# Attention loop: the last three query units' projections in one or two chunks a step, and their later stages moved

## The chip, the cores and the metric

The kernel runs on one core of a Trainium2 chip. Its time is the device time of one execution in microseconds (us); the figure quoted is the median of the runs. The core has a matmul engine (TensorE, PE in the profile), a vector engine (VectorE, DVE), an activation engine (ScalarE, ACT), a general engine (GpSimd, POOL) and a queue engine that issues the transfers (SyncE, SP). Each runs its own instructions strictly in the order written, and they meet at semaphores.

## What is computed

Two layers on a sequence of 512 tokens with 1024 features. The first has a gated short convolution, the second differential attention on a shared key and value set; each ends with a squared-ReLU MLP. The change lies in the attention of the second layer:

```python
q = rms_norm((h @ w_q).reshape(b, s, 8, 2, 64), q_norm)          # 8 heads, two components of 64
for i in range(s // 128):                                        # 4 blocks of 128 queries
    sc = einsum('bqhcd,bkhcd->bhcqk', qb, kb) * scale            # both components
    p = softmax(where(causal, sc, NEG_INF))
    a = p[:, :, 0] - lam * p[:, :, 1]
    out = einsum('bhqk,bkhe->bqhe', a, vb)
o = rms_norm(o, sub_norm) * (1 - lam_init)
return o.reshape(b, s, 1024) @ w_o
```

## The kernel before

Everything is float32. A large product is made of three passes, a high part times a high part, high times low and low times high, so one chunk (128 of the 1024 features that are summed over) is three matmuls of 128x512. Weights arrive by transfer in `w_raw`, ACT makes the high part (`w_hi`, L843) and DVE the rest (`w_lo`, L1148); this pair is called a split.

**The steps.** The attention is a loop over `STEPS` = 32 steps, n = 4h + i, with head h and query block i. Each engine has its own copy of the loop with its own order, written by hand, and the work of neighbouring steps is interleaved. In step n, PE does `scores(n+2)` (L739, and L742 for the mask), then filler matmuls, then `values(n-1)` (L761), then transposes of queries or of a finished head, then `weights_T(n)` (L751), the transposes of the softmax weights. ACT does `exps(n+1)` (L1070) and `evacuate(n)` (L1078), which copies the transposed weights out of PSUM, and at i = 0 `copy_o(h-1)` (L1085, L1086), the copy and square of a finished head's output. DVE does `row_max(n+2)` (L1512) and `weights(n+1)` (L1520 to L1527), and the norm of a finished head: `out_ms` (L1533 on), `out_norm` (L1544) and `out_lo` (L1548). ACT's `out_hi` (L1090) goes before `out_lo`. PE cannot begin `scores(m)` before `exps(m-2)` is done.

**The query units.** The projection h @ w_q is cut into 8 units of 8 chunks. Unit u = 4..7 belongs to query block u - 4 of heads 4 to 7. Units 0 to 4 are projected before the loop. Units 5, 6 and 7 are projected inside it and serve as PE's filler. Each unit goes through these stages:

- `project(u)` on PE (L700), into the one PSUM bank `B_Q`. The next unit's first chunk waits until the bank has been read.
- `take_q(u)` on ACT (L1047 copy, L1050 square), which empties the bank.
- `q_stats(u)` on DVE (L1480, L1483), a power on POOL (L432), `q_norm_part(u)` on DVE (L1491).
- `queries_T(u)` on PE (L720), four transposes into the PSUM bank `B_T`, then `q_hi(u)` on ACT (L1055) and `q_lo(u)` on DVE (L1500), which empty it.

`out_T(h)` (L773), the transposes of a finished head, uses the same bank `B_T`, which `out_hi` and `out_lo` empty. It runs at i = 3 of the next head. `scores(16)` to `scores(19)`, the first of head 4, need units 4 to 7, so `q_lo(7)` has to be done before `scores(19)`, which PE issues in step 17.

**What fills PE afterwards.** The output projection's first block, `project_out(0, chunk)` (L470), is put into single steps by the table `WO_FILL`. It uses bank `B_Q` too. The table `WO_EARLY` puts four splits of its weights at the end of steps 11, 15, 18 and 22.

Of the kernel before, what the change touches and what calls it, by code (L numbers as in the profile page):

```python
# [30 lines left out]
KC = D // P  # L31
# [16 lines left out]
Q_BANK = (4, 5, 0, 1, B_Q, B_Q, B_Q, B_Q)  # L48
QT_BANK = (B_T, B_O, B_T, B_O, B_T, B_T, B_T, B_T)
STEPS = 4 * H  # L50
WO_FILL = {(3, 1): (0,), (3, 2): (1,), (4, 1): (2,), (5, 1): (3,), (6, 1): (4,), (7, 1): (5,)}
WO_EARLY = {(2, 3): 0, (3, 3): 1, (4, 2): 2, (5, 2): 3}
K_T_AFTER = 7
X_BANK = (4, 5, 6, 7, 2, 3, 4, 5)
# [19 lines left out]
I_A, I_Z, I_M0, I_KV, I_Q, I_O, I_M1 = range(7)  # L74
# [48 lines left out]
def build(nc, x, a_norm, a_w_in, a_conv, a_w_out, kv_norm, w_kv, k_norm, b_norm, w_q, q_norm,  # L123
          lam_q1, lam_k1, lam_q2, lam_k2, sub_norm, w_o, mlp_norm, w_up, w_down, out):
    with ExitStack() as ctx:
# [274 lines left out]
        @block.gpsimd  # L400
        def _(pool):
            nc.gpsimd.memset(ident[:], 0.0).then_inc(s_zero, 1)
            nc.gpsimd.memset(maskb[:], 0.0).then_inc(s_zero, 1)
            pool.wait_ge(s_zero, 2)
            nc.gpsimd.affine_select(out=ident[:], in_=ident[:], compare_op=ALU.not_equal, fill=1.0, base=0,
                                    pattern=[[-1, P]], channel_multiplier=1).then_inc(s_zero, 1)
            nc.gpsimd.affine_select(out=maskb[:], in_=maskb[:], compare_op=ALU.is_ge, fill=NEG, base=0,
                                    pattern=[[-1, P]], channel_multiplier=1).then_inc(s_zero, 1)
            nc.gpsimd.memset(mhalf[:], -0.5).then_inc(s_zero, 1)

            def norm(i):

                if i > NORM_A:
                    pool.wait_ge(s_nst, i)
                    if i == NORM_B:
                        pool.wait_ge(s_xlo, PRODUCTS * NQ - 1)
                    nc.gpsimd.memset(sqsum, 0.0).then_inc(s_zero, 1)
                    pool.wait_ge(s_zero, 5 + i)
                    for m in range(KC):
                        pool.wait_ge(s_sq, 8 * i + m + 1)  # L420
                        nc.gpsimd.tensor_tensor(sqsum, sqsum, sqb[m % 2], ALU.add).then_inc(s_add, 1)
                        pool.wait_ge(s_add, 8 * i + m + 1)
                pool.wait_ge(s_nms, i + 1)
                nc.gpsimd.tensor_tensor(rcol[:, i, :], nms[:, i, :], mhalf[:, 0:TB], ALU.pow).then_inc(s_nrc, 1)

            norm(NORM_A)
            norm(NORM_M0)
            norm(NORM_B)

            def q_power(u):  # L430
                pool.wait_ge(s_qms, u + 1)
                nc.gpsimd.tensor_tensor(qpw[:, u, :], qms[:, u, :], mhalf[:, 0:8], ALU.pow).then_inc(s_qrs, 1)  # L432

            def out_power(h):
                pool.wait_ge(s_oms, h + 1)
                if h:
                    pool.wait_ge(s_on, h)
                nc.gpsimd.tensor_tensor(ors[:], oms[:], mhalf[:, 0:TB], ALU.pow).then_inc(s_ors, 1)

            for g in range(2):  # L440
                pool.wait_ge(s_kms, g + 1)
                nc.gpsimd.tensor_tensor(k_rs[:, g, :], k_ms[:, g, :], mhalf[:], ALU.pow).then_inc(s_krs, 1)
            for u in range(5):
                q_power(u)
            for h in range(H):
                if h:
                    out_power(h - 1)
                if h < 3:
                    q_power(5 + h)
            out_power(H - 1)  # L450
            norm(NORM_M1)

# [2 lines left out]
        def _(pe):  # L455
# [233 lines left out]
            def project(u, ks):  # L689

                t = u - 4
                if 0 in ks and u == 4:
                    pe.wait_ge(s_kg, H)
                elif 0 in ks:
                    pe.wait_ge(s_qsq, 2 * u)
                for k in ks:
                    n = S_Q + 4 + k // 2
                    wait_slab(n)
                    for i, (half, w) in enumerate(((0, w_hi), (0, w_lo), (1, w_hi))):
                        last = nc.tensor.matmul(ps[:, B_Q, :], h1[:, half, k, t * P:(t + 1) * P],  # L700
                                                w[:, slot(n), (k % 2) * T:(k % 2 + 1) * T],
                                                start=(k == 0 and i == 0), stop=(k == KC - 1 and i == 2))
                    if u == 7 and k % 2 == 1:
                        last.then_inc(s_used, 1)
                    elif u < 7 and k == KC - 1:
                        last.then_inc(s_qp, 1)

            def queries_T(u):

                pe.wait_ge(s_qn, u + 1)  # L710
                if u == 0:
                    pe.wait_ge(s_kg, H)
                elif u == 1:
                    pe.wait_ge(s_qsq, 4)
                else:
                    pe.wait_ge(s_qlo, u - 1 if u < 4 else u)
                if u >= 6:
                    pe.wait_ge(s_lo, 8 * I_O + u - 5)
                for hh in range(4):
                    last = nc.tensor.transpose(ps[:, QT_BANK[u], hh * P:(hh + 1) * P],  # L720
                                               q_nrm[u % 2][:, hh * P:(hh + 1) * P], ident[:])
                last.then_inc(s_qT, 1)
# [42 lines left out]
            def out_T(h):  # L765

                pe.wait_ge(s_on, h + 1)
                if h < 3:
                    pe.wait_ge(s_qlo, h + 6)
                if h:  # L770
                    pe.wait_ge(s_lo, 8 * I_O + h)
                for i in range(TB):
                    last = nc.tensor.transpose(ps[:, B_T, i * P:(i + 1) * P], o_sb[:, i * P:(i + 1) * P], ident[:])  # L773
                last.then_inc(s_oT, 1)
# [16 lines left out]
            for n in range(STEPS):  # L791
                h, i = divmod(n, 4)
                if n + 2 < STEPS:
                    scores(n + 2)
                if h < 3 and i < 3:
                    project(5 + h, (range(0, 3), range(3, 6), range(6, KC))[i])
                if (h, i) == (3, 1):
                    pe.wait_ge(s_qsq, 16)
                if (h, i) in WO_FILL:
                    project_out(0, WO_FILL[h, i])  # L800
                if (h, i) == (H - 1, 2):
                    pe.wait_ge(s_exp, 2 * STEPS - 2)
                    project_out(1, range(0, 3))
                if (h, i) == (H - 1, 3):
                    project_out(1, range(3, 5))
                if n:
                    values(n - 1)
                if i == 2 and h < 4:
                    queries_T(4 + h)
                if i == 3 and h:  # L810
                    out_T(h - 1)
                weights_T(n)
# [21 lines left out]
        def _(act):  # L834
# [217 lines left out]
            def q_hi(u):  # L1052
                act.wait_ge(s_qT, u + 1)
                g, t = divmod(u, 4)
                nc.scalar.activation(h2[:, 0, 4 * g:4 * g + 4, t * P:(t + 1) * P],  # L1055
                                     ps[:, QT_BANK[u], :].rearrange("p (h q) -> p h q", h=4), ACT.Copy,
                                     scale=hgs[:, 0:1]).then_inc(s_qhi, 1)
# [47 lines left out]
            for n in range(STEPS):  # L1105
                h, i = divmod(n, 4)
                if n + 1 < STEPS:
                    exps(n + 1)
                if i == 0 and h:
                    copy_o(h - 1)  # L1110
                if i == 2 and h < 4:
                    q_hi(4 + h)
                if i == 3 and h < 3:
                    take_q(5 + h)
                evacuate(n)
                if i == 3 and h:
                    out_hi(h - 1)
                if (h, i) in WO_EARLY:
                    split(S_WO + WO_EARLY[h, i])
# [15 lines left out]
        def _(dve):  # L1135
# [435 lines left out]
            for n in range(STEPS):  # L1571
                h, i = divmod(n, 4)
                if i == 0 and h >= 2:
                    out_lo(h - 2)
                if n + 2 < STEPS:
                    row_max(n + 2)
                if i == 1 and h:
                    out_ms(h - 1)
                if n + 1 < STEPS:
                    weights(n + 1)  # L1580
                if i == 1 and h < 4:
                    q_norm_part(4 + h)
                if i == 2 and h:
                    out_norm(h - 1)
                if i == 2 and h < 4:
                    q_lo(4 + h)
                if i == 3 and h < 3:
                    q_stats(5 + h)
                if (h, i) in WO_EARLY:
                    split(S_WO + WO_EARLY[h, i])  # L1590
            out_lo(H - 2)
# [34 lines left out]
```

## Time and profile before

| | us |
|---|---|
| median of 3 runs | 1119.24 (1118.9 to 1120.17) |
| the profiled execution | 1118.9 |
| its span in the trace | 1117.1 |
| attention loop: first of its scores to the tail of the output projection | about 644 to 754 |
| PE busy | 1097.7 (98%) |
| DVE busy | 793.6 (71%) |
| ACT busy | 478.9 (43%) |
| POOL busy | 78.6 (7%) |

The span is what the trace shows between the first and the last instruction; 1.8 us of the execution lie around it. A timeline row gives the start, the duration, the engine, the line and the tiles, and in brackets the idle time of the engine before it with what ended it. An engine can begin its next instruction before the previous one's recorded end, so the cost of an instruction in a chain is the distance between starts.

### The profile page before, as it was taken

To read this page: it belongs to the slowest core of one execution; us is meant where nothing else is said; L and a number is where in the kernel's file an instruction comes from. 1 tells how busy PE (TensorE), PEld (TensorE's weight loads), DVE (VectorE), ACT (ScalarE), POOL (GpSimd) and SP (SyncE) were. 2 spreads that over 40 slices of the span, in tenths; PEclk is the share of its full clock that TensorE was granted. 3 is DMA by queue.
4 is the path that set the end of the run, shared out by engine and by line. 5 is a ranking of instruction groups with operands and counts; after the bars stand their busy time and mean duration, and the time that the engine had idled before them with its cause. 6 is when DMAs were issued, how large, how long until landed. Compare 5 with 4: busy or idle time off the path is not lost.

```text
span 1117.1 us, 13426 instructions
## 1 busy us (share of the span) xinstructions
PE 1097.7 (98%) x5176; PEld 903.8 (81%) x5176; DVE 793.6 (71%) x988; ACT 478.9 (43%) x695; POOL 78.6 (7%) x58
## 2 busy tenths in 40 slices
PE   9999999999999999999999998899999999999998
PEld 7788888888888888888888876677878888888887
DVE  5766554787787787688664678946668678678686
ACT  6221224353353353355532366834544344344343
POOL 0000012000000000002510211013100000000000
PEclk9999999999999999999999999999999999999999
DMA  7433463314315315201322300142323423414302
GB/s 189 93 98 99 131 208 95 113 38 155 109 38 173 91 41 186 76 1 57 114 94 76 113 1 20 58 151 78 113 74 110 117 76 116 127 59 139 88 1 75
DMA packets 144752, 105.90 MB, mean 95 GB/s; under 512 B 12592, under 2 KB 121136, under 8 KB 144688
## 3 DMA queue, kind: packets, MB, share of 16 engines
q1 hardware_dynamic: 143648, 105.03, 30.7%
q8 instruction: 41, 0.67, 0.3%
q14 instruction: 23, 0.19, 0.1%
q10 hardware_dynamic: 1040, 0.00, 0.1%
HBM read 102.93 MB, written 2.10 MB: 94 GB/s over the span
## 4 chain that ended last, share of the span: by engine, by line
PE 94%; DVE 3%; issue 1%; ACT 1%; POOL 0%; ACTq 0%; DVEq 0%; POOLq 0%
PE ps L588 31%; PE ps L615 27%; PE ps L470 18%; PE ps L675 10%; PE ps L700 2%; PE ps L761 1%; DVE nmax L1512 1%; PE ps L739 1%; PE ps L751 0%; ACT w_hi L843 0%; PE ps L523 0%; DVE h L1548 0%; PE ps L720 0%; PE ps L557 0%; PE ps L649 0%
## 5 line engine op out<-in xcount | busy, mean ns | idle before, releaser
L588 PE MATMUL ps<-h,w_hi 128*128 128x512 f32 x1024 | 316.3, 390 | 0.0
L615 PE MATMUL ps<-w_hi,h 128*128 128x512 f32 x896 | 277.6, 389 | 0.8 <-ACT kv L932 0.8
L588 PEld LDWEIGHTS ps<-h,w_hi 128*128 128x128 f32 x1024 | 191.6, 188 | 39.3
L470 PE MATMUL ps<-h,w_hi 128*128 128x512 f32 x640 | 199.1, 392 | 3.4 <-DVE w_lo L1148 1.6
L588 PE MATMUL ps<-h,w_lo 128*128 128x512 f32 x512 | 199.4, 389 | 0.0
L615 PEld LDWEIGHTS ps<-w_hi,h 128*128 128x128 f32 x896 | 168.2, 188 | 36.0 <-issue 1.0
L615 PE MATMUL ps<-w_lo,h 128*128 128x512 f32 x448 | 174.4, 389 | 0.0
L470 PEld LDWEIGHTS ps<-h,w_hi 128*128 128x128 f32 x640 | 118.8, 188 | 28.6 <-DVE h L1548 1.8
L928 ACT ACTIVATE w_hi<-b_raw 128x1024 fp32r<-128x1024 f32 x80 | 82.1, 1055 | 137.6 <-PE ps L588 78.1
L470 PE MATMUL ps<-h,w_lo 128*128 128x512 f32 x320 | 124.7, 390 | 0.0
L1249 DVE TENSOR_TENSOR w_lo<-b_raw,w_hi 128x1024 fp32r<-128x1024 f32 x80 | 95.9, 1224 | 27.4 <-ACT w_hi L928 27.4
L588 PEld LDWEIGHTS ps<-h,w_lo 128*128 128x128 f32 x512 | 96.1, 188 | 20.2
L1148 DVE TENSOR_TENSOR w_lo<-w_raw,w_hi 128x1024 fp32r<-128x1024 f32 x67 | 85.7, 1283 | 32.7 <-ACT w_hi L843 31.8
L1256 DVE SCALAR_TENSOR_TENSOR work<-ps,rB 128x512 f32<-128x512 f32 x64 | 44.3, 691 | 84.0 <-PE ps L588 72.0
L675 PE MATMUL ps<-w_hi,h 128*128 128x512 f32 x320 | 101.6, 393 | 0.0
L615 PEld LDWEIGHTS ps<-w_lo,h 128*128 128x128 f32 x448 | 84.1, 188 | 17.3
L843 ACT ACTIVATE w_hi<-w_raw 128x1024 fp32r<-128x1024 f32 x67 | 69.7, 1052 | 65.8 <-DMA w_raw<-in_a_w_in 26.3
L928 ACT ACTIVATE w_hi<-w_raw 128x1024 fp32r<-128x1024 f32 x60 | 62.6, 1054 | 71.0 <-DMA w_raw<-in_w_up 50.4
L1249 DVE TENSOR_TENSOR w_lo<-w_raw,w_hi 128x1024 fp32r<-128x1024 f32 x60 | 72.7, 1219 | 15.9 <-ACT w_hi L928 15.9
L1314 DVE TENSOR_TENSOR kv<-ps,kv 128x512 f32<-128x512 f32 x104 | 69.6, 687 | 18.3 <-PE ps L615 17.6
L939 ACT ACTIVATE a_raw<-work 128x512 f32<-128x512 f32 x64 | 40.1, 626 | 97.8 <-DVE work L1256 97.8
L470 PEld LDWEIGHTS ps<-h,w_lo 128*128 128x128 f32 x320 | 60.1, 188 | 12.6
(133 smaller groups left out, 1196.7 us busy)
## 6 DMA issues: line engine op xcount, KB each, us to landing
b_raw<-in_w_down SPq DMA_DIRECT2D x64, 512.0 KB, 4.5
w_raw<-in_w_up SPq DMA_DIRECT2D x64, 512.0 KB, 4.1
w_raw<-in_a_w_in SPq DMA_DIRECT2D x23, 512.0 KB, 3.8
w_raw<-in_w_kv SPq DMA_DIRECT2D x16, 512.0 KB, 3.7
w_raw<-in_a_w_out SPq DMA_DIRECT2D x8, 512.0 KB, 4.2
w_raw<-in_w_q SPq DMA_DIRECT2D x8, 512.0 KB, 3.5
w_raw<-in_w_o SPq DMA_DIRECT2D x8, 512.0 KB, 4.0
kv<-in_x SPq DMA_DIRECT2D x4, 512.0 KB, 6.5
```

The lines of the kernel that those rows point to most:

```text
L470: last = nc.tensor.matmul(ps[:, bank, :], w[:, s, k * P:(k + 1) * P], src(half, k), start=(k == 0 and i == 0), stop=(k == KC - 1 and i == 2))
L588: last = nc.tensor.matmul(ps[:, v % 4, :], w[:, s_, k * P:(k + 1) * P], h_of[inp][:, half, k, :], start=(k == 0 and i == 0), stop=(k == KC ...
L615: last = nc.tensor.matmul(ps[:, CHAIN[p][tb], :], op[half][:, k, tb * P:(tb + 1) * P], w[:, s_, cols], start=(FRESH[p] and k == 0 and i == ...
L675: last = nc.tensor.matmul(ps[:, use % KV_BANKS, :], tok[:, half, k, t * P:(t + 1) * P], w[:, s, k2 * T:(k2 + 1) * T], start=(pos == 0 and ...
L700: last = nc.tensor.matmul(ps[:, B_Q, :], h1[:, half, k, t * P:(t + 1) * P], w[:, slot(n), (k % 2) * T:(k % 2 + 1) * T], start=(k == 0 and ...
L843: nc.scalar.activation(w_hi[:, slot(n), :], w_raw[:, n % RAW, :], ACT.Copy).then_inc(s_whi, 1)
L928: nc.scalar.activation(w_hi[:, slot(entry(q, e)), :], src, ACT.Copy).then_inc(s_whi, 1)
L939: nc.scalar.activation(a_raw[:, j, :], r_up[j % 2], ACT.Square).then_inc(s_asq, 1)
L1148: V.tensor_tensor(w_lo[:, slot(n), :], w_raw[:, n % RAW, :], w_hi[:, slot(n), :].bitcast(F32), ALU.subtract).then_inc(s_wlo, 1)
L1249: V.tensor_tensor(w_lo[:, slot_, :], src, w_hi[:, slot_, :].bitcast(F32), ALU.subtract).then_inc(s_wlo, 1)
L1256: V.scalar_tensor_tensor(r_up[j % 2], ps[:, v % 4, :], 0.0, rB[:], ALU.max, ALU.mult).then_inc(s_up, 1)
L1314: V.tensor_tensor(part, ps[:, CHAIN[p][tb], :], part, ALU.add).then_inc(s_dv, 1)
```

## The change

It sets where each piece of units 4 to 7 stands in the four loops. Nothing is added or removed: the same 24 chunks, the same copies, norms and transposes run, in another order. In steps:

| stage | before | after |
|---|---|---|
| chunks of units 5, 6, 7 | 3, 3, 2 in steps 0-2, 4-6, 8-10 | unit 5: 2, 2, 2, 1, 1 in steps 0-4; unit 6: the same in 5-9; unit 7: 2, 2, 2, 2 in 10-13 |
| `take_q` of 5, 6, 7 | 3, 7, 11 | 4, 9, 13 |
| `q_stats` of 5, 6, 7 | 3, 7, 11 | 5, 10, 14 |
| `q_norm_part` of 4, 5, 6, 7 | 1, 5, 9, 13 | 1, 6, 11, 15 |
| `queries_T`, `q_hi`, `q_lo` of 4, 5, 6, 7 | 2, 6, 10, 14 | 2, 7, 12, 16 |
| output chunks 0, 1, 2 of `WO_FILL` | 13, 14, 17 | 15, 17, 18 |

The core of the diff:

```diff
-WO_FILL = {(3, 1): (0,), (3, 2): (1,), (4, 1): (2,), (5, 1): (3,), (6, 1): (4,), (7, 1): (5,)}
+WO_FILL = {(3, 3): (0,), (4, 1): (1,), (4, 2): (2,), (5, 1): (3,), (6, 1): (4,), (7, 1): (5,)}
+Q_STEPS = {0: (5, 0, 2), 1: (5, 2, 4), 2: (5, 4, 6), 3: (5, 6, 7), 4: (5, 7, 8),
+           5: (6, 0, 2), 6: (6, 2, 4), 7: (6, 4, 6), 8: (6, 6, 7), 9: (6, 7, 8),
+           10: (7, 0, 2), 11: (7, 2, 4), 12: (7, 4, 6), 13: (7, 6, 8)}
+Q_TAKEN, Q_SUMMED = {4: 5, 9: 6, 13: 7}, {5: 5, 10: 6, 14: 7}
+Q_SCALED, Q_TURNED = {1: 4, 6: 5, 11: 6, 15: 7}, {2: 4, 7: 5, 12: 6, 16: 7}
...
                 if u >= 6:
-                    pe.wait_ge(s_lo, 8 * I_O + u - 5)
+                    pe.wait_ge(s_lo, 8 * I_O + u - 4)
...
                 pe.wait_ge(s_on, h + 1)
-                if h < 3:
-                    pe.wait_ge(s_qlo, h + 6)
+                if h in (0, 2, 3):
+                    pe.wait_ge(s_qlo, (6, 0, 7, 8)[h])
...
-                if h < 3 and i < 3:
-                    project(5 + h, (range(0, 3), range(3, 6), range(6, KC))[i])
-                if (h, i) == (3, 1):
+                if n in Q_STEPS:
+                    u, first, last = Q_STEPS[n]
+                    project(u, range(first, last))
+                if (h, i) == (3, 3):
                     pe.wait_ge(s_qsq, 16)
...
-                if i == 2 and h < 4:
-                    queries_T(4 + h)
+                if n in Q_TURNED:
+                    queries_T(Q_TURNED[n])
```

ACT and DVE test the same tables in the same places of their loops. POOL makes unit 5's power after head 0's instead of before it, and so on for 6 and 7.

The first place is PE at steps 4 and 5 (`ps<-w_hi,h` and `ps<-w_lo,h` are chunks of a projection, `ps<-kv,work` is `values`, `ps<-ident,kv` is `weights_T`, `ps<-ah,h` is `scores`). Before, step 4 begins unit 6, whose bank was emptied in step 3:

```order
L742 MATMUL ps<-maskb,identb 128x128 x2
L700 MATMUL ps<-w_hi,h 128x512
L700 MATMUL ps<-w_lo,h 128x512
L700 MATMUL ps<-w_hi,h 128x512 x2
L700 MATMUL ps<-w_lo,h 128x512
L700 MATMUL ps<-w_hi,h 128x512 x2
L700 MATMUL ps<-w_lo,h 128x512
L700 MATMUL ps<-w_hi,h 128x512
L761 MATMUL ps<-kv,work 128x128 x4
L751 MATMUL ps<-ident,kv 128x128
```

After, in the same place, step 4 ends unit 5 with one chunk, and step 5 begins unit 6:

```order
L705 MATMUL ps<-w_hi,h 128x512
L705 MATMUL ps<-w_lo,h 128x512
L705 MATMUL ps<-w_hi,h 128x512
L766 MATMUL ps<-kv,work 128x128 x4
L756 MATMUL ps<-ident,kv 128x128
L744 MATMUL ps<-ah,h 128x512 x6
L747 MATMUL ps<-maskb,identb 128x128 x2
L705 MATMUL ps<-w_hi,h 128x512
L705 MATMUL ps<-w_lo,h 128x512
L705 MATMUL ps<-w_hi,h 128x512 x2
```

Between the last chunk of one unit and the first of the next there are now one `values`, one `weights_T` and one `scores`; before, there was a whole step without chunks.

The second place is PE at step 7 (the first `ps<-ident,work` is `queries_T`, the second `out_T`). Before, `queries_T` stands in step 6 and `out_T` in step 7:

```order
L761 MATMUL ps<-kv,work 128x128 x2
L720 MATMUL ps<-ident,work 128x128 x4
L751 MATMUL ps<-ident,kv 128x128 x3
L739 MATMUL ps<-ah,h 128x256 x6
L742 MATMUL ps<-maskb,identb 128x128 x2
L761 MATMUL ps<-kv,work 128x128 x3
L773 MATMUL ps<-ident,work 128x128 x4
```

After, both stand in step 7, one right behind the other:

```order
L766 MATMUL ps<-kv,work 128x128 x3
L725 MATMUL ps<-ident,work 128x128 x4
L778 MATMUL ps<-ident,work 128x128 x4
L756 MATMUL ps<-ident,kv 128x128 x4
L744 MATMUL ps<-ah,h 128x384 x6
```

Nothing of PE's is left between the two users of bank `B_T`.

The third place is DVE at steps 15 to 17. Before (`w_lo` is the split, `h<-ps,hgs,h 128x512` is `out_lo`, `nmax<-ps` is `row_max`):

```order
L1148 TENSOR_TENSOR w_lo<-w_raw,w_hi 128x1024
L1548 SCALAR_TENSOR_TENSOR h<-ps,hgs,h 128x512
L1512 TENSOR_REDUCE nmax<-ps 128x2
L1520 RECIPROCAL rinv<-rsum 128x1
L1522 TENSOR_SCALAR rinv<-rinv,rsum,lams 128x1
L1527 SCALAR_TENSOR_TENSOR kv<-kv,rinv 128x256
L1512 TENSOR_REDUCE nmax<-ps 128x2
```

After:

```order
L1154 TENSOR_TENSOR w_lo<-w_raw,w_hi 128x1024
L1554 SCALAR_TENSOR_TENSOR h<-ps,hgs,h 128x512
L1518 TENSOR_REDUCE nmax<-ps 128x2
L1526 RECIPROCAL rinv<-rsum 128x1
L1528 TENSOR_SCALAR rinv<-rinv,rsum,lams 128x1
L1533 SCALAR_TENSOR_TENSOR kv<-kv,rinv 128x256
L1506 SCALAR_TENSOR_TENSOR h<-ps,hgs,h 128x4x128
L1518 TENSOR_REDUCE nmax<-ps 128x2
```

`q_lo(7)` now stands between `weights(17)` and `row_max(19)`, and the scores that `row_max(19)` reads wait for it.

## Rows read from the trace of the kernel before

**Rows 1.** The page: the span, and the chain that ended last, by engine.
```profile
span 1117.1 us, 13426 instructions
...
PE 94%; DVE 3%; issue 1%; ACT 1%; POOL 0%; ACTq 0%; DVEq 0%; POOLq 0%
```
**Rows 2.** Windows: stretch, its length, busy PE, PEld, DVE, ACT, POOL, clock, transfers.
```profile
657.00:671.00 14.00, 13.95 (x100) 11.05 (x96) 11.01 (x26) 8.63 (x26) 2.64 (x2) 1.00 0.00 1
...
685.00:698.00 13.00, 9.84 (x74) 7.43 (x74) 11.28 (x25) 8.53 (x25) 2.64 (x2) 1.00 0.14 42
...
721.00:731.00 10.00, 8.64 (x70) 6.45 (x69) 9.15 (x23) 7.21 (x24) 1.01 (x1) 1.00 0.17 52
```
**Rows 3.** Timeline of PE in head 3: start, duration, then idle before.
```profile
687.46 0.97 PE L739 MATMUL ps<-ah,h 64*128 64x512 f32 x6 [1.13 <-ACT kv L1070]
...
690.23 0.44 PE L751 MATMUL ps<-ident,kv 128*128 128x128 f32 x2 [0.61 <-DVE kv L1527]
...
693.93 0.66 PE L720 MATMUL ps<-ident,work 128*128 128x128 f32 x4 [1.30 <-DVE work L1491]
```
**Rows 4.** Timeline of PE, step 4, then steps 8 and 9.
```profile
657.46 0.48 PE L700 MATMUL ps<-w_hi,h 128*128 128x512 f32 x1
...
671.27 0.47 PE L700 MATMUL ps<-w_hi,h 128*128 128x512 f32 x1
...
673.43 1.05 PE L761 MATMUL ps<-kv,work 128*128 128x128 f32 x8
...
674.52 0.96 PE L739 MATMUL ps<-ah,h 64*128 64x512 f32 x6
...
675.51 0.47 PE L700 MATMUL ps<-w_hi,h 128*128 128x512 f32 x1
```
**Rows 5.** Timeline of ACT: take_q of unit 6, then copy_o and evacuate of step 8.
```profile
669.23 0.61 ACT L1047 ACTIVATE kv<-ps 128x512 f32<-128x512 f32 x1
669.71 0.62 ACT L1050 ACTIVATE work<-ps 128x512 f32<-128x512 f32 x1
...
674.52 0.60 ACT L1085 ACTIVATE work<-ps 128x512 f32<-128x512 f32 x1 [1.88 <-PE ps L761]
...
675.49 0.29 ACT L1078 ACTIVATE work<-ps 128x128 f32<-128x128 f32 x1
```
**Rows 6.** Timeline of all engines: loop start, and bank B_T used in step 2.
```profile
643.25 0.75 DVE L1500 SCALAR_TENSOR_TENSOR h<-ps,hgs,h 128x512 fp32r<-128x512 f32 x1 [0.74 <-ACT h L1055]
...
644.15 0.79 PE L739 MATMUL ps<-ah,h 64*128 64x384 f32 x6 [0.44 <-DVE h L1500]
...
653.57 0.60 PE L720 MATMUL ps<-ident,work 128*128 128x128 f32 x4
...
654.01 0.49 PE L751 MATMUL ps<-ident,kv 128*128 128x128 f32 x3
654.21 0.69 ACT L1055 ACTIVATE h<-ps,hgs 128x512 fp32r<-128x512 f32 x1 [1.36 <-PE ps L720]
...
654.93 0.75 DVE L1500 SCALAR_TENSOR_TENSOR h<-ps,hgs,h 128x512 fp32r<-128x512 f32 x1 [0.80 <-ACT h L1055]
```
**Rows 7.** Timeline of all engines, steps 15 to 17.
```profile
697.20 0.60 PE L751 MATMUL ps<-ident,kv 128*128 128x128 f32 x4
...
697.84 0.60 ACT L1078 ACTIVATE work<-ps 128x512 f32<-128x512 f32 x1 [1.45 <-PE ps L751]
698.33 0.68 ACT L1090 ACTIVATE h<-ps,hgs 128x512 fp32r<-128x512 f32 x1
...
698.90 1.06 ACT L843 ACTIVATE w_hi<-w_raw 128x1024 fp32r<-128x1024 f32 x1
...
699.99 1.23 DVE L1148 TENSOR_TENSOR w_lo<-w_raw,w_hi 128x1024 fp32r<-128x1024 f32 x1 [1.99 <-ACT w_hi L843]
...
700.92 0.96 PE L739 MATMUL ps<-ah,h 64*128 64x512 f32 x6 [1.12 <-ACT kv L1070]
701.13 0.74 DVE L1548 SCALAR_TENSOR_TENSOR h<-ps,hgs,h 128x512 fp32r<-128x512 f32 x1
...
703.60 1.23 DVE L1512 TENSOR_REDUCE nmax<-ps 128x2 f32<-128x1024 f32 x1
```

More of the change, by code:

```diff
@@ L447, in _ @@
                     out_power(h - 1)
-                if h < 3:
-                    q_power(5 + h)
+                if 1 <= h < 4:
+                    q_power(4 + h)
             out_power(H - 1)
@@ L767, in out_T @@
                 pe.wait_ge(s_on, h + 1)
-                if h < 3:
-                    pe.wait_ge(s_qlo, h + 6)
+                if h in (0, 2, 3):
+                    pe.wait_ge(s_qlo, (6, 0, 7, 8)[h])
                 if h:
@@ L1110, in _ @@
                     copy_o(h - 1)
[L1111 to L1114, printed above, removed]
+                if n in Q_TURNED:
+                    q_hi(Q_TURNED[n])
+                if n in Q_TAKEN:
+                    take_q(Q_TAKEN[n])
                 evacuate(n)
@@ L1580, in _ @@
                     weights(n + 1)
-                if i == 1 and h < 4:
-                    q_norm_part(4 + h)
+                if n in Q_SCALED:
+                    q_norm_part(Q_SCALED[n])
                 if i == 2 and h:
                     out_norm(h - 1)
[L1585 to L1588, printed above, removed]
+                if n in Q_TURNED:
+                    q_lo(Q_TURNED[n])
+                if n in Q_SUMMED:
+                    q_stats(Q_SUMMED[n])
                 if (h, i) in WO_EARLY:
```

## The prediction

> **What bounds the kernel now.** I first read the page's chain: PE makes 94% of it [rows 1], and outside the attention PE hardly waits, so all that an order in the attention can change is PE's pauses there. Then the busy time by stretch. In head 1 PE is busy 13.95 of 14.00 us: heads 0 to 2 are bound by PE, which has the unit projections as extra work. In head 3 PE is busy 9.84 of 13.00 us and in head 5 8.64 of 10.00, while DVE is busy 9.15 of 10.00 there: from head 3 on, the chain through DVE and ACT sets the pace [rows 2]. The timeline of PE names the pauses of head 3: 1.13, 0.61 and 1.30 us, then 1.12 before `scores(19)` [rows 3, 7]. So the change takes chunks from the stretch that PE bounds (heads 0 to 2 have 20 of the 24 instead of all) and gives four to head 3. Alone, four chunks at 0.7 us would be worth up to 2.9 us.
>
> **Unit costs.** Distances between starts. Three chunks take 2.16 us (671.27 to 673.43), so a chunk is 0.69 and each group 0.09 more; `values` of four blocks and one `weights_T` take 1.09 (673.43 to 674.52); the widest `scores` with its mask 0.99 (674.52 to 675.51) [rows 4]. On ACT, `take_q` is 0.48 to its square, the square ends 0.62 later; `copy_o` begins 1.09 after its `values` began and takes 0.97 to the next instruction [rows 4, 5]. A use of bank `B_T` costs: 0.64 from `queries_T` to `q_hi`, 0.72 to `q_lo`, 0.90 from `q_lo` to the PE instruction that waits for it, against 0.44 for the transposes alone [rows 6].
>
> **PE's time to `scores(19)`, before.** That instruction begins at 700.92, and the loop's first scores at 644.15 [rows 6, 7]: 56.8 us. How much of that is work? A head's period in the bound stretch is 13.81 us (657.46 to 671.27) [rows 4]; its chunks take 2 x 2.16 + 1.47 = 5.8, its two transposes 0.9, and I put short waits for `evacuate` at 0.35 (an estimate), so 6.8 us remain for scores, values and weight transposes. To `scores(19)` this gives 4 x 6.8, less 0.9 (no `values` in step 0), plus 1.9 for step 16, 1.3 + 1.8 for transposes, 17.3 for 24 chunks and 1.6 for two output chunks: 50.2. The pauses are then 6.6 us, of which 4.2 have rows.
>
> **After: the new pauses, in order.** I follow the instructions with the unit costs.
> (a) Step 5. Unit 6's first chunk waits for `take_q(5)`, which now stands in step 4, behind `copy_o(0)`. From the start of `values(3)`: 1.09 + 0.97 + 0.48 + 0.62 + 0.1 to the semaphore = 3.2 us, while PE has 1.09 + 0.99 = 2.1 to do. Pause 1.1. Behind the waiting chunk are `values(4)` and `weights_T(5)`, and ACT waits for them. Before, step 3 had no chunks and hid `take_q`.
> (b) Step 7. `out_T(0)` stands right behind `queries_T(5)` and must find `B_T` empty: 0.64 + 0.72 + 0.90 = 2.26 less 0.44. Pause 1.8. Before, a `weights_T`, a `scores` and a `values` lay between them.
> (c) Step 10. `take_q(6)` without a `copy_o` in front, but behind `exps(10)`: 0.35.
> (d) Step 12. `queries_T(6)` waits for `out_lo(1)`, which stands behind the split of step 11. The same chain stands in rows 7 for step 15: from the start of `weights_T` 0.64 to `evacuate`, 0.49, 0.57, 1.09 to the DVE part, 1.14 to `out_lo`, 0.9 to PE: 4.8 us. PE has 0.5 + 0.8 + 1.5 + 0.9 = 3.7 to do (`weights_T`, `scores`, two chunks, `values`). Pause 1.0 (it was 1.13 [rows 3]).
> (e) Steps 13 to 15. `take_q(7)` stands before `evacuate(13)`, and DVE's weights for step 14 come late: 0.4 + 0.35 + 0.1 = 0.9 (before 0.6 + 1.3).
> (f) Step 16. `queries_T(7)` waits for `out_lo(2)` by the same 4.8 us, but PE has only 0.5 + 0.8 + 0.9 = 2.2 to do, since no chunk stands there. Pause 2.5.
> (g) Step 17. `scores(19)` needs `q_lo(7)`. `queries_T(7)` begins at about 700.9, `q_lo(7)` must let `row_max(18)` and `weights(17)` pass on DVE and ends near 703.3. PE has `weights_T(16)` alone. Pause 1.9.
> The sum is 9.6 us, 3.0 more than before. The work is 50.2 less one output chunk that now stands behind (0.8) plus 0.3 for more groups: 49.7. So `scores(19)` begins at 644.15 + 49.7 + 9.6 = 703.4, against 700.92: 2.5 us later.
>
> **What of that reaches the end.** From here DVE sets the pace. Before, DVE took up these scores at 703.60 [rows 7], though they begin at 700.92 and their result is there 1.22 us later, at 702.14 (0.99 of issue and the drain of the mask): 1.46 us of slack. So DVE's `row_max(19)` comes at 703.4 + 1.2 = 704.65 instead of 703.60, 1.06 us late. `q_lo(7)` (0.67 us of DVE) lies inside DVE's wait. In heads 4 to 6 DVE has next to no gap, so nothing is made up, and the tail of the output projection is PE's again and simply starts later. The output chunk moved from step 14 to 17 and 17 to 18 falls into PE's pauses of over 1 us. I add 0.15 for PE's slow restart behind a pause (an estimate: the two chunk groups behind pauses in the new order cost 0.09 each). The moved transfers are none: the splits and slabs stay in their steps, and the slab that the first split needs is released in step 10 instead of 8, ahead of step 11. POOL's powers have a step to pass.
>
> Profiled execution: 1118.9 + 1.2 = 1120.1. Its time lies 0.3 under the median shown, so for the median 1119.24 + 1.2 = 1120.4 us.
>
> **Bounds.** For the pauses (a) and (b) the lower end is nothing and the upper end the whole hand-over (3.2 and 2.3); I keep the difference to PE's own work, because the order leaves nothing else between. For (f) and (g) together the lower end is 1.5 (the slack eats the rest and the change is nil), the upper end 4.4 with no slack, because ACT's `evacuate(16)` is late too: 3.5 us late at the end.
>
> One rule of the Trainium skill speaks against the change (Perfetto Trace Analysis, section Optimizing Tensor Performance): independent matmul groups should rotate through several PSUM banks, so that one group's evacuation overlaps the next one's matmuls. Units 5 to 7 share one bank, and `B_T` has two users. The rows agree in so far as the emptying of `B_T` takes 2.26 us against 0.44 of transposes [rows 6]; by the rule every such meeting costs its evacuation, which is what (a), (b) and (f) say.
>
> **Rivals.**
> Faster: the chunks pay. If (a) and (b) do not appear, PE reaches step 8 2.9 us earlier, DVE and ACT with it, and the whole chain of head 3 shifts: 1.2 - 2.9 = -1.7, so 1117.5. It decides from the point where (a) and (b) together are under 1.7 us. For it: PE was 100% busy there, so each chunk taken away counts [rows 2]. Against it: both costs are fixed durations in an order that leaves PE nothing else to do [rows 5, 6]. The Trainium skill says in the same page (section Identifying Performance Opportunities) that interleaving stretches with different bounds may help; by it the 2.9 us would be the gain. Chance 0.10.
> No difference: DVE's lateness at step 17 is under 0.5 us because the split of step 15 (PE is then about 1 us ahead) is early and `q_lo(7)` slips in front. 1119.3. Chance 0.20.
> Slower by more: no slack in step 17. `evacuate(16)` stands behind `q_hi(7)` on ACT, and `weights(17)` to `weights(19)` drift, so nearly the 2.5 us and another pause of about 0.8 in step 18 arrive. 1119.24 + 3 = 1122.3. Chance 0.17.
> The clock falls: granted clock is 1.00 in each stretch [rows 2], which is 2.4 GHz, with pauses up to 1.30 [rows 3]; the new ones are 2.5 and 1.9 within 7 us. If it fell to 1.2 GHz for one head, PE's 8.64 us would be 17.3 in a period of 10: 7 us more, 1127. Chance 0.02.
> The Trainium skill (TensorE: Matmul & The Clock Gate, section HAM oscillation) says that long idle gaps return the clock to half; no gap of this trace's attention did so.
> The forecast itself, 1119.7 to 1121.2, has 0.51.
>
> **How the numbers follow.** Less than 0.2%, 2.24 us, a measurement of this kernel cannot tell from no change. The forecast, the case of no difference and most of the faster one lie inside: 0.73. Slower by over 0.2% means over 1121.5: the third rival, the clock and the upper edge of the forecast, 0.21. Faster means under 1117.0, which asks for more than the first rival gives: 0.06. The range that leaves 2 in 10 out is 1118.1 to 1122.6.
>
> **What would show it.** Right: in the changed kernel's timeline PE's first chunk behind the widest scores of step 5 has about 1.1 us of idle before it, released by ACT's square; `out_T(0)` about 1.8, released by DVE; `queries_T(7)` about 2.5, released by `out_lo`; `scores(19)` about 1.9, released by `q_lo`. DVE idles over 1 us before `row_max(19)`, and heads 4 to 6 keep their period of about 10.15. Wrong: a pause of (a) or (b) under half its size, or heads 4 to 6 with another period, or a granted clock under 1.00.

## The result, and the profile after

The changed kernel takes 1122.68 us (median of 8 runs, 1121.61 to 1123.23), against 1119.25 for the kernel before in the same series: ratio 1.003, 95% interval 1.0021 to 1.0039. It is 3.4 us slower where 1.2 was forecast, just outside the range (1118.1 to 1122.6).

The page, with the span that answers to [rows 1]:

```profile
span 1120.8 us, 13426 instructions
```

The windows of the changed kernel over the stretches of [rows 2], and the one in between; the third number from the right is the granted clock:

```profile
657.00:671.00 14.00, 11.41 (x80) 9.03 (x79) 10.13 (x24) 7.09 (x22) 2.64 (x2) 1.00 0.00 1
...
685.00:698.00 13.00, 11.63 (x85) 8.97 (x84) 11.40 (x25) 9.47 (x27) 2.29 (x2) 1.00 0.14 42
698.00:711.00 13.00, 8.98 (x46) 6.69 (x45) 9.65 (x20) 6.80 (x19) 1.36 (x2) 0.74 0.14 41
...
721.00:731.00 10.00, 8.65 (x70) 6.46 (x69) 9.67 (x22) 8.31 (x24) 1.01 (x1) 1.00 0.18 52
```

Head 1, where PE was busy 13.95 of 14.00 us [rows 2], now has 2.6 us of idle, and the granted clock of 698 to 711 is 0.74. Here is PE's timeline; these are all its marked pauses between the loop's first scores and `scores(19)`, with the first behind it:

```profile
644.00 0.79 PE L744 MATMUL ps<-ah,h 64*128 64x384 f32 x6 [0.45 <-DVE h L1506]
...
660.34 0.50 PE L705 MATMUL ps<-w_hi,h 128*128 128x512 f32 x1 [0.93 <-ACT work L1056]
...
670.38 0.63 PE L778 MATMUL ps<-ident,work 128*128 128x128 f32 x4 [1.66 <-DVE h L1506]
...
687.86 0.63 PE L725 MATMUL ps<-ident,work 128*128 128x128 f32 x4 [0.96 <-DVE h L1554]
...
692.60 0.71 PE L766 MATMUL ps<-kv,work 128*128 128x128 f32 x4 [0.25 <-ACT work L1084]
...
693.93 0.62 PE L744 MATMUL ps<-ah,h 64*128 64x256 f32 x6 [0.17 <-ACT kv L1076]
...
701.28 0.63 PE L725 MATMUL ps<-ident,work 128*128 128x128 f32 x4 [2.34 <-DVE h L1554]
...
703.71 1.65 PE L744 MATMUL ps<-ah,h 64*128 64x512 f32 x6 [1.69 <-DVE h L1506]
...
720.70 0.55 PE L756 MATMUL ps<-ident,kv 128*128 128x128 f32 x3 [1.32 <-DVE kv L1533]
```

The pauses of [rows 3] are gone; those named (a), (b), (d), (f) and (g) stand in their place with the releasers that the prediction named. `scores(19)` begins at 703.71 (forecast: 703.4; before: 700.92 [rows 7]). From the start of the loop that is 59.71 us against 56.77; the windows of just these two stretches give PE's busy time, first before, then after:

```profile
644.15:700.92 56.77, 52.32 (x363) 40.66 (x364) 45.20 (x101) 36.57 (x107) 9.56 (x7) 1.00 0.04 11
```

```profile
644.00:703.71 59.71, 51.53 (x362) 40.09 (x362) 47.92 (x106) 38.71 (x113) 9.56 (x7) 0.99 0.06 19
```

But `scores(19)` lasts 1.65 us, where the same six matmuls lasted 0.96. The windows of one us around it say why; the first number behind the length is PE's busy time, the third from the right the granted clock:

```profile
701.00:702.00 1.00, 0.72 (x5) 0.53 (x5) 1.00 (x3) 0.15 (x2) 0.00 (x0) 1.00 0.29 84
702.00:703.00 1.00, 0.02 (x1) 0.00 (x0) 0.93 (x4) 1.00 (x3) 0.00 (x0) 1.00 0.98 291
703.00:704.00 1.00, 0.29 (x2) 0.33 (x4) 0.56 (x1) 0.93 (x4) 0.00 (x0) 0.53 0.53 158
704.00:705.00 1.00, 1.00 (x6) 0.56 (x4) 0.00 (x0) 0.00 (x0) 0.00 (x0) 0.50 0.00 0
...
708.00:709.00 1.00, 1.00 (x9) 0.78 (x9) 0.81 (x2) 1.00 (x4) 0.89 (x1) 0.50 0.00 0
709.00:710.00 1.00, 1.00 (x5) 0.82 (x4) 0.68 (x3) 0.68 (x3) 0.00 (x0) 0.55 0.00 0
710.00:711.00 1.00, 1.00 (x9) 0.81 (x7) 0.96 (x3) 0.00 (x0) 0.00 (x0) 1.00 0.00 0
```

At 703, in the second of two long pauses, the granted clock falls from 1.00 to 0.50, from 2.4 to 1.2 GHz, and stays there to about 709.9. The two pauses had PE idle for 2.34 and 1.69 us with 0.7 us of transposes between them. DVE's and ACT's timelines show how a slow PE gets onto their chain:

```profile
705.72 1.23 DVE L1518 TENSOR_REDUCE nmax<-ps 128x2 f32<-128x1024 f32 x1 [2.16 <-PE ps L747]
...
709.23 0.42 DVE L1518 TENSOR_REDUCE nmax<-ps 128x2 f32<-128x256 f32 x1 [0.39 <-PE ps L747]
...
712.60 1.23 DVE L1154 TENSOR_TENSOR w_lo<-w_raw,w_hi 128x1024 fp32r<-128x1024 f32 x1 [1.02 <-ACT w_hi L849]
...
715.77 0.94 DVE L1518 TENSOR_REDUCE nmax<-ps 128x2 f32<-128x768 f32 x1
```

```profile
707.96 0.38 ACT L1084 ACTIVATE work<-ps 128x256 f32<-128x256 f32 x1 [4.03 <-PE ps L756]
...
711.13 0.49 ACT L1084 ACTIVATE work<-ps 128x384 f32<-128x384 f32 x1 [1.45 <-PE ps L756]
711.52 1.05 ACT L849 ACTIVATE w_hi<-w_raw 128x1024 fp32r<-128x1024 f32 x1
```

The kernel before has these two rows where the changed one has 711.52 and 715.77:

```profile
707.75 1.05 ACT L843 ACTIVATE w_hi<-w_raw 128x1024 fp32r<-128x1024 f32 x1
```

```profile
712.00 0.95 DVE L1512 TENSOR_REDUCE nmax<-ps 128x2 f32<-128x768 f32 x1
```

`row_max(19)` starts 2.12 us later than before (703.60 [rows 7]). The next delay comes through ACT: the split of step 18 stands behind `evacuate(18)`, which waits for `weights_T(18)`, which a slow PE reaches at 710.60. DVE waits 1.02 us for it. From there DVE has no gap until the first step of head 7 (735.29), where one of 1.0 us stood before too, and nothing is given back: that row also is 3.76 us later than before.

### The profile page after: what moved, and what is told of

Same layout as the page of the kernel before. It is cut to its first block, busy times and chain, and to the rows that moved or that the text cites. A ratio compares the mean times of both kernels' runs of the same rounds, so it can differ in the third digit from the quotient of the medians.

```text
span 1120.8 us, 13426 instructions
## 1 busy us (share of the span) xinstructions
PE 1099.0 (98%) x5176; PEld 905.1 (81%) x5176; DVE 793.6 (71%) x988; ACT 479.0 (43%) x695; POOL 78.6 (7%) x58
## 4 chain that ended last, share of the span: by engine, by line
PE 94%; DVE 3%; ACT 2%; issue 1%; POOL 0%; ACTq 0%; POOLq 0%; DVEq 0%
PE ps L593 31%; PE ps L620 27%; PE ps L475 19%; PE ps L680 10%; PE ps L705 2%; PE ps L744 1%; PE ps L766 1%; DVE nmax L1518 1%; PE ps L756 1%; ACT w_hi L849 0%; PE ps L528 0%; DVE h L1554 0%; PE ps L747 0%; PE ps L562 0%; PE ps L575 0%
```

## The experiments

A matmul "of no use" below is one of the identity matrix (0.22 us), written where the next real result overwrites it. The ratios are to the kernel before on the same chip. The interval of each is about 0.001 either way, that is 1.1 us, so differences of 1 us between two of the kernels rest on the ranges of their runs and on the timelines. The kernel before itself has two groups of times, which the mean clock of the runs sorts (last part of this section).

**Both long pauses filled (warm_both).**

```diff
+                if m == 19:                      # scores(19), ahead of its wait for q_lo(7)
+                    for _ in range(6):
+                        nc.tensor.matmul(ps[:, 2 * b, 0:P], ident[:], ident[:], start=True, stop=True)
...
+                if n == 16:                      # ahead of queries_T(7)
+                    for _ in range(8):
+                        nc.tensor.matmul(ps[:, B_AT, 0:P], ident[:], ident[:], start=True, stop=True)
```

> The changed kernel with work of no use added for PE in its two longest pauses: 8 matmuls 128x128 of the identity matrix (about 0.22 us each by the rows) before queries_T(7) in step 16 and 6 before scores(19) in step 17. Nothing waits for them and their results are overwritten. Theory 1 (clock): the order itself costs about 1.1 to 1.3 us, and the rest of the 3.4 us is PE running at 1.2 GHz from about 703.5 to 709.6 because of these pauses; with PE kept at work the granted clock stays 1.00 and the time is about 1120.4, 2.3 under the changed kernel. Theory 2 (chain): the low clock costs little since DVE and ACT set the pace there, and the missing 2.3 us come from evacuate(16) and the weights falling behind; then the clock reads 1.00 but the time stays at 1122.3 or more.

1120.32 us (1120.16 to 1120.55), ratio 1.0009 (1.0 to 1.0018), mean clock 1.000 in all 11 runs. More work for PE makes the kernel 2.4 us faster than the changed one, and the runs of the two do not overlap (1121.61 is the lowest there). In its windows (same columns) the clock is 1.00 over the stretch that was at 0.50, and `scores(19)` is back to its length though it starts where it did (this execution's loop lies 0.24 us later):

```profile
703.89 0.96 PE L747 MATMUL ps<-ah,h 64*128 64x512 f32 x6 [0.26 <-DVE h L1512]
```

```profile
703.00:704.00 1.00, 0.74 (x8) 0.55 (x7) 0.84 (x2) 1.00 (x5) 0.00 (x0) 1.00 0.88 264
704.00:709.00 5.00, 4.95 (x37) 3.61 (x39) 3.71 (x11) 2.05 (x8) 1.01 (x1) 1.00 0.02 5
```

DVE takes up the scores of step 17 at 705.11, 1.5 us later than before, and its row 713.50, which answers to 715.77 above and to 712.00 before, is 1.5 late too:

```profile
705.11 1.23 DVE L1524 TENSOR_REDUCE nmax<-ps 128x2 f32<-128x1024 f32 x1 [1.27 <-PE ps L750]
...
713.50 0.95 DVE L1524 TENSOR_REDUCE nmax<-ps 128x2 f32<-128x768 f32 x1
```

So the order costs 1.4 us (1120.32 against 1118.92 beside it; against the runs of the kernel before that kept the clock, 1118.70 to 1119.36, there is no overlap), and the clock 2.4. Theory 2 is refuted.

**One pause filled (warm16, warm17).** Each has one half of the edit above.

> The changed kernel with only the 8 matmuls of no use before queries_T(7) in step 16; the pause before scores(19), 1.69 us, stays. Which pause lets the clock fall? If the sum of both counts: clock 1.00 and 1120.3, as with both filled. If the second alone is enough: clock 0.997 and about 1122.5. In between (it falls in some executions): a spread of times between these two.

> The changed kernel with only the 6 matmuls of no use before scores(19); the pause before queries_T(7), 2.34 us, stays. If the sum counts: clock 1.00 and 1120.3. If the longest pause decides: clock under 1.00, the low stretch begins nearer to it, 1121 to 1122.7.

warm16: 1121.65 us, ratio 1.0017 (1.0008 to 1.0026); 3 of 11 runs have a mean clock of 1.000 (1120.37 to 1120.52), 8 have 0.998 (1121.45 to 1122.06). warm17: 1120.34 us, ratio 1.0013 (1.0004 to 1.0022); 7 of 11 have 0.999 or 1.000 (1120.10 to 1120.34), 4 have 0.998 (1121.42 to 1121.60). With neither filled, none of 8 runs kept the clock, with both, all 11 did. Filling the pause before `scores(19)` clearly helps: none of 8 against 7 of 11 without the other filled, 3 of 11 against all 11 with it filled. That the first pause counts too rests on less: none of 8 against 3 of 11, and 7 against all 11; and 3 against 7 of 11 is no clear difference. What the numbers do show is that the longest single pause does not sort the runs. In warm16 no pause of this place is longer than the one below, and 8 of 11 runs lost the clock; in warm17 one of 2.34 us was left, and 4 of 11 did.

```profile
704.38 1.65 PE L744 MATMUL ps<-ah,h 64*128 64x512 f32 x6 [1.69 <-DVE h L1509]
```

The expectation of warm16 named this outcome, "in between"; that of warm17 did not have it. Between 698.95 and 703.71 the changed kernel's PE does nothing but five transposes; whether transposes hold the clock as other matmuls do, no run here separates.

**One output chunk into the pause (fill16).**

```diff
-WO_FILL = {(3, 3): (0,), (4, 1): (1,), (4, 2): (2,), (5, 1): (3,), ...
+WO_FILL = {(3, 3): (0,), (4, 0): (1,), (4, 1): (2,), (5, 1): (3,), ...
```

> The changed kernel with output chunks 1 and 2 one step earlier (steps 16 and 17 instead of 17 and 18): chunk 1 fills 0.78 us of the pause before queries_T(7). Theory 1: scores(19) begins where it did, the pause is 1.6 instead of 2.3, and if that is enough for the clock to stay, about 1120.2; if the clock falls all the same, about 1122. Theory 2: 1122.3, since no step of the DVE and ACT chain moves.

1121.83 us (1121.14 to 1122.09), ratio 1.0019 (1.001 to 1.0028), clock 0.997 or 0.998 in all runs. The pause is 1.65 instead of 2.34, and the clock falls all the same, in the profiled run later and for a shorter time:

```profile
698.00:711.00 13.00, 9.65 (x65) 7.08 (x62) 9.83 (x21) 8.32 (x22) 1.98 (x2) 0.87 0.14 41
```

That is the 1122 of theory 1's second case; it does not tell the theories apart by itself, since theory 2 said 1122.3.

**queries_T(5) at the front of step 7 (turn5_early).**

```diff
+                if n in (7,):
+                    queries_T(Q_TURNED[n])
                 if n in Q_STEPS:
...
-                if n in Q_TURNED:
+                if n in Q_TURNED and n not in (7,):
```

> The changed kernel with queries_T(5) at the front of step 7, ahead of unit 6's two chunks and values(6), which then stand between the two users of bank B_T. Theory 1: pause (b), 1.66 us, goes to under 0.2, PE bounds this stretch, so everything behind comes 1.5 us earlier; the two long pauses and the fall of the clock stay: about 1121.1. Rival: the chain of DVE and ACT in head 3 sets the pace and (b) is absorbed in it: 1122.6, no change.

1120.97 us (1119.87 to 1121.56), ratio 1.0013 (1.0005 to 1.0022): 1.7 less than the changed kernel. The pause before `out_T(0)` is gone and the later ones are the same size, 1.3 us earlier:

```profile
686.55 0.63 PE L725 MATMUL ps<-ident,work 128*128 128x128 f32 x4 [0.95 <-DVE h L1556]
...
699.98 0.63 PE L725 MATMUL ps<-ident,work 128*128 128x128 f32 x4 [2.34 <-DVE h L1556]
...
702.40 1.65 PE L744 MATMUL ps<-ah,h 64*128 64x512 f32 x6 [1.69 <-DVE h L1508]
```

Pause (b) is therefore a full cost, and the fall of the clock is another.

**take_q(5) ahead of copy_o(0) (take5_first).**

```diff
                     exps(n + 1)
+                if n == 4:
+                    take_q(5)
                 if i == 0 and h:
                     copy_o(h - 1)
...
-                if n in Q_TAKEN:
+                if n in Q_TAKEN and n != 4:
```

> The changed kernel with take_q(5) ahead of copy_o(0) on ACT in step 4, and nothing else. If pause (a), 0.93 us, is a cost by itself: it goes, everything behind comes 0.9 earlier, 1121.8, the clock falls as before. If it hides a wait behind it (q_stats and POOL's power for unit 5, as seen when queries_T(5) was also moved up): 1122.0 to 1122.7.

1121.53 us (9 runs, 1120.53 to 1122.11), ratio 1.0019 (1.001 to 1.0029). The runs overlap those of the changed kernel, so the time alone would not carry it; the timeline does: the pause at 660.34 is gone and `scores(19)` starts at 702.74 instead of 703.71, though this loop starts 0.16 us later. Pause (a) is a cost by itself.

**Both of these with the pauses filled (early_and_warm).**

> Three edits of the changed kernel together: take_q(5) ahead of copy_o(0) on ACT in step 4, queries_T(5) at the front of step 7, and both long pauses filled with matmuls of no use. Theory 1: pauses (a) 0.93 and (b) 1.66 go, PE bounds there, so the time is 1120.3 - 0.9 - 1.5 = 117.9 over 1000, that is 1117.9, clock 1.00: 1.0 under the kernel before. Rival: the chain of DVE and ACT from step 11 on absorbs the gain: 1119.5 to 1120.3.

1118.53 us, ratio 0.9992 (0.9983 to 1.0001), clock 1.000 in 10 of 11 runs and 0.999 in one. 0.6 more than expected: with both edits PE comes to `queries_T(5)` before `q_norm_part(5)` is done, which waits for POOL's power. The saved 0.93 us come back as a pause of 0.95 there:

```profile
666.03 0.66 PE L725 MATMUL ps<-ident,work 128*128 128x128 f32 x4 [0.95 <-DVE work L1507]
```

**Unit 7 one step earlier (turn7_step15).**

```diff
-Q_TAKEN, Q_SUMMED = {4: 5, 9: 6, 13: 7}, {5: 5, 10: 6, 14: 7}
-Q_SCALED, Q_TURNED = {1: 4, 6: 5, 11: 6, 15: 7}, {2: 4, 7: 5, 12: 6, 16: 7}
+Q_TAKEN, Q_SUMMED = {4: 5, 9: 6, 13: 7}, {5: 5, 10: 6, 13: 7}
+Q_SCALED, Q_TURNED = {1: 4, 6: 5, 11: 6, 14: 7}, {2: 4, 7: 5, 12: 6, 15: 7}
...
+                if n in (15,):
+                    queries_T(Q_TURNED[n])
                 if n in Q_STEPS:
```

> The changed kernel with unit 7's late stages one step earlier (q_stats 13, norm 14, queries_T, q_hi and q_lo 15), and queries_T(7) at the front of step 15, ahead of the output chunk and values. It no longer waits for out_lo(2), and scores(19) no longer waits for q_lo(7). Theory 1: pauses (f) and (g), 2.34 and 1.69 us in the trace, become one of about 1.1 for exps(17) and one under 0.5 before out_T(2); clock 1.00; about 1118.7, at or a little under the kernel before. Theory 2 (the low clock is harmless, the chain lost at steps 5 to 12 is what counts): about 1121.

1122.24 us, ratio 1.0025 (1.0016 to 1.0034). A miss by 3.5 us. Of its 10 runs 4 have a clock of 0.999 or 1.000 (1121.43 to 1121.63) and 6 have 0.998 (1122.23 to 1122.64), so even with the clock kept this order is 1.2 us slower than warm_both. The edit brought a wait that I had not counted, the same one as above: PE stands at `queries_T(7)` for 1.82 us, since the norm waits for POOL's 1.64 us of power.

```profile
696.74 0.66 PE L725 MATMUL ps<-ident,work 128*128 128x128 f32 x4 [1.82 <-DVE work L1499]
```

The new wait spoils the comparison, and the number decides nothing between the theories.

**Unit 7 in its own bank (own_bank), and the same with the pause filled (own_bank_warm).**

```diff
-QT_BANK = (B_T, B_O, B_T, B_O, B_T, B_T, B_T, B_T)
+QT_BANK = (B_T, B_O, B_T, B_O, B_T, B_T, B_T, B_Q)
-WO_FILL = {(3, 3): (0,), (4, 1): (1,), (4, 2): (2,), (5, 1): (3,), (6, 1): (4,), (7, 1): (5,)}
+WO_FILL = {(4, 1): (0,), (4, 2): (1,), (5, 1): (2,), (5, 2): (3,), (6, 1): (4,), (7, 1): (5,)}
-Q_TAKEN, Q_SUMMED = {4: 5, 9: 6, 13: 7}, {5: 5, 10: 6, 14: 7}
+Q_TAKEN, Q_SUMMED = {4: 5, 9: 6, 13: 7}, {5: 5, 10: 6, 13: 7}
...
+                if u == 7:
+                    pe.wait_ge(s_qsq, 16)
...
+                if n == 16:                      # PE, front of the step; wait: take_q(7) done
+                    queries_T(Q_TURNED[n])
...
+                    if n == 7:                   # PE: between unit 6's two chunks
+                        project(u, range(first, first + 1))
+                        queries_T(Q_TURNED[n])
+                        first = first + 1
...
+                if n == 4:                       # ACT, ahead of copy_o
+                    take_q(5)
+                if n == 16:
+                    q_hi(7)
...
+                if n == 16:                      # DVE, ahead of row_max(18)
+                    q_lo(7)
```

> Unit 7's transposes go to the projection's own bank B_Q, free after take_q(7), at the front of step 16, so they wait neither for out_lo(2) nor sit behind weights(17): q_hi(7) stands ahead of copy_o(3), q_lo(7) ahead of row_max(18). Output chunks 0 to 3 move to steps 17, 18, 21, 22, since they use that bank. take_q(5) ahead of copy_o(0), queries_T(5) between unit 6's two chunks of step 7. No useless matmuls. Order alone: row_max(19) at about 701.4 against 703.60 before, so 1118.85 - 2.2 = 1116.7 with the clock at 1.00. But PE has only scores and values in step 16 and then waits near 2 us for scores(19): if the clock falls there, 1118 to 1119.

> own_bank with matmuls of no use in its pause: 3 before weights_T(16), 6 before scores(19). If order and clock are the whole story: 1116.7 with the clock at 1.00 in every run, 2.2 under the kernel before. If the chain behind step 17 has another bound: 1118.5 as early_and_warm.

own_bank: 1117.48 us, ratio 0.9988 (0.998 to 0.9997). 7 of 11 runs have clock 1.000 (1117.26 to 1117.64), 4 have 0.998 (1118.30 to 1118.74). own_bank_warm: 1117.48 us (1117.26 to 1117.56), ratio 0.9985 (0.9977 to 0.9994), clock 1.000 in all 11. Both beat the kernel before (its fastest run beside them is 1118.57) and the changed one, but lie 0.8 us above the 1116.7 expected with the clock kept. This is one edit made of several: unit 7's own bank and early place, its `q_stats` in step 13, `take_q(5)` first, `queries_T(5)` inside step 7 and the output chunks moved. What each gives is not separated. PE still waits 2.29 us for `scores(19)`, but 3.3 us sooner than in the changed kernel, and DVE takes the scores up at 701.98, 1.6 before [rows 7] (0.6 later than I expected):

```profile
700.42 0.96 PE L746 MATMUL ps<-ah,h 64*128 64x512 f32 x6 [2.29 <-DVE h L1516]
```

```profile
701.98 1.23 DVE L1528 TENSOR_REDUCE nmax<-ps 128x2 f32<-128x1024 f32 x1
```

**The kernel before and its clock (before_warm, before_warm_head4).** The kernel before ran 97 times beside the experiments, and its times fall into two groups: in the series beside own_bank, 24 of 32 runs have a mean clock of 1.000 and 1118.57 to 1119.21 us, 8 have 0.997 or 0.998 and 1119.98 to 1120.73.

```diff
+                if m == 15:                      # before_warm: head 3
+                    pe.wait_ge(s_qsq, 16)
+                    for _ in range(4):
+                        nc.tensor.matmul(ps[:, B_Q, 0:P], ident[:], ident[:], start=True, stop=True)
...
+                if u == 7:
+                    pe.wait_ge(s_qlo, u)
+                    pe.wait_ge(s_lo, 8 * I_O + u - 5)
+                    for _ in range(5):
+                        nc.tensor.matmul(ps[:, B_T, 0:P], ident[:], ident[:], start=True, stop=True)
```

```diff
+                if n in (17, 18):                # before_warm_head4: ahead of weights_T
+                    pe.wait_ge(s_ev, n)
+                    for _ in range(2 if n == 17 else 5):
+                        nc.tensor.matmul(ps[:, B_AT, 0:P], ident[:], ident[:], start=True, stop=True)
```

> The kernel before the change with matmuls of no use in two pauses of head 3: 4 before scores(15) and 5 before queries_T(7). Of its 32 runs beside the first experiments, 23 have a mean granted clock of 1.000 and times of 1118.7 to 1119.4, and 9 have 0.997 or 0.998 and 1119.8 to 1120.9. Theory 1: that second group is the same fall of the clock after head 3's pauses; filled, all runs read 1.000 and lie at 1118.7 to 1119.4. Rival: the second group comes from another place or has another cause, and about one run in four stays near 1120.2.

> The kernel before with 2 matmuls of no use before weights_T(17) and 5 before weights_T(18), where the trace with a fallen clock shows pauses of 0.58 and 1.36 behind one of 1.13. Filling head 3's pauses left 5 of 11 runs at 0.998. Theory: the fall comes from the pauses of 700 to 707, so all runs read 1.000 here and lie at 1118.7 to 1119.1. Rival: it is still head 3 together with head 4, and a part of the runs stays at 0.998 and about 1120.

before_warm: 1119.02 us, ratio 1.0002 (0.9994 to 1.0011); 5 of 11 runs still at 0.997 or 0.998, so the rival held for the place. Its profiled run is one of them and shows where the clock falls, in head 4's pauses:

```profile
703.56 0.44 PE L760 MATMUL ps<-ident,kv 128*128 128x128 f32 x2 [0.58 <-DVE kv L1536]
...
706.63 0.90 PE L760 MATMUL ps<-ident,kv 128*128 128x128 f32 x3 [1.36 <-DVE kv L1536]
```

```profile
705.00:706.00 1.00, 0.27 (x3) 0.08 (x1) 0.89 (x6) 1.00 (x4) 0.39 (x1) 1.00 0.00 0
706.00:707.00 1.00, 0.37 (x2) 0.38 (x3) 0.97 (x3) 0.16 (x2) 0.62 (x1) 0.76 0.00 0
707.00:708.00 1.00, 1.00 (x7) 0.67 (x7) 0.95 (x3) 0.44 (x2) 0.00 (x0) 0.50 0.00 0
```

With these filled instead, before_warm_head4 has 1.000 in all 11 runs: 1118.77 us (1118.62 to 1119.34), ratio 0.9997 (0.9988 to 1.0005). The kernel before fell in 29 of its 97 runs, so 11 in a row without a fall would be chance about once in 50. The second group of the kernel before is the clock, at 1.2 to 1.3 us.

## Why the prediction was wrong

**Right in the main: the order and its pauses.** Step by step, forecast and trace: (a) 1.1 and 0.93; (b) 1.8 and 1.66; (d) 1.0 and 0.96; (e) 0.9 and 0.42 marked; (f) 2.5 and 2.34; (g) 1.9 and 1.69; (c), 0.35, has no marked row. That (a) and (b) reach the end in full is shown by turn5_early (1.7 us less) and, less sharply, by take5_first (1.15 less). So the "faster" rival fell at the point it named: (a) and (b) together are 2.6, not under 1.7.

**Partly luck: PE's time to `scores(19)`.** I had 59.3 us, the trace has 59.7 (644.00 to 703.71), but the two parts of the sum are off in opposite directions: 49.7 of work and 9.6 of pauses, where the windows have 51.5 busy and 8.2 idle. The same split was wrong for the kernel before: 50.2 and 6.6, where they have 52.3 and 4.5. So the "pauses without rows" that I inferred there, 2.4 us, hardly exist. The largest part is the estimate of 0.35 us a head for short waits, 1.4 over four heads, which [rows 2] did not bear out: PE was busy 13.95 of 14.00.

**Right within 0.2 us: what the order costs at the end.** The sum said 1.06, and 0.15 for PE's restarts; with the clock held at 1.00 the same order costs 1.40 (warm_both). There `row_max(19)` is 1.5 us late where the sum had 1.06, since `scores(19)` begins that much later than forecast. DVE's wait at `scores(19)` there is 1.27, as the text's "over 1 us".

**Wrong: the clock.** This is the step that failed: the sum has no term for it, so it stands there at nothing. The prediction had it only as a rival with a chance of 0.02 and a price of 7 us, on the ground that the granted clock was 1.00 in each stretch of the one trace and that its pauses went up to 1.30. It fell in each of the 8 runs (mean clock 0.996 to 0.998), for 6.8 us in the profiled one, and cost 2.4. A granted clock under 1.00 was also one of the signs of being wrong that the prediction named. Two errors lie behind the 0.02. I judged by the longest single pause, though the new ones stand together, 2.34 and 1.69 with 0.7 us of work between, and the longest does not sort the runs (warm16 and warm17). And I took one trace with 1.00 as proof that the old pauses were harmless, where the kernel before already loses its clock in 29 of 97 runs. It was near the edge, and I could have read that in part from the spread of its three times, 1118.9 to 1120.17. The rule that I cited from the Trainium skill (TensorE: Matmul & The Clock Gate, section HAM oscillation) and set aside names the mechanism: by it, long idle gaps return the clock to half. The trace agrees in so far as the windows show 1.00 before the two pauses and 0.50 behind them.

**The price.** A PE at half its clock matters although DVE sets the pace there. It made `scores(19)` 0.7 us longer, so that `row_max(19)` is 2.12 us late, of which the order alone makes 1.5 (warm_both); and it took PE's slack of head 4 away, so that the split of step 18 came late through ACT. DVE's row at 715.77 is 3.77 us behind, of which warm_both again keeps 1.5. The 7 us of the rival were too many because it had the clock low for a whole head; it was low for 6.8 us, and part of that fell on slack.

**The "slower by more" rival** gave 1122.3 and so the nearest number, but that is luck: its mechanism is another (no slack in step 17, without the clock). warm_both refutes it: DVE's delay there is 1.5 and stays so.

## What to carry to other kernels

Work moved off a bound engine gains only what its hand-overs leave. Here a unit's bank has to be emptied between its last chunk and the next unit's first one (a pause of 0.93 us), and two users of one bank side by side cost nearly the whole emptying (1.66 us in step 7). Look for the place where the next user waits, and put the moved work, or another bank, there. And look at PE's neighbouring pauses together, not only at the longest one: if a kernel's times already fall into two groups with different mean clocks, it stands at the edge, and a change that adds pauses can cost the clock as well. Here it did in 8 of 8 runs.

## What the runs showed of the hardware

- Fourteen matmuls of no use, 3.1 us of PE work, made the changed kernel 2.4 us faster, by holding the clock at 1.00.
- The fall is a matter of chance at the edge: none, 3, 7 and all of the runs kept the clock (of 8, 11, 11, 11) as no pause, the first, the second and both were filled. The kernel before, whose pauses there are 1.12, 0.58 and 1.38 us, lost it in 29 of 97, and own_bank, whose longest there is 2.29, in 4 of 11. Which run falls is not explained by anything in its order.
- Once down, the clock stayed at 0.50 although PE was then busy throughout. By windows of 1 us it was low for 6.8 us in the changed kernel (703.1 to 709.9) and in turn5_early, for 3.4 us in before_warm (706.5 to 709.9), in fill16 and in warm16 (0.50 in whole windows, the ends from the part of a window that was low). The longer kind goes with the 2.4 us of the changed kernel, the shorter with the 1.2 to 1.3 us between the two groups of the kernel before. What decides between the two lengths, these runs do not settle.
